# Low-part products last in each half slot, a finer first slot, and turns moved by one product, in a two-layer encoder trunk

## The chip, the core and the metric

The kernel runs on one core of a Trainium2 chip. The metric is the device time of one execution in microseconds (us); the figure for a kernel is the median of its runs. Engines: TensorE (PE; its weight loads are PEld), VectorE (DVE), ScalarE (ACT), GpSimd (POOL), and the DMA queue of SyncE (SP).

## What is computed

An encoder trunk on x of 256 tokens by 2048 features, in float32:

```python
hn = rms_norm(h, mix_norm_g[0]);  h = h + diff_hgrn_mixer(hn, ab_w_in, ab_w_out, ...)   # 8+8 heads
hn = rms_norm(h, mlp_norm_g[0]);  h = h + square(relu(hn @ mlp_w_up[0])) @ mlp_w_down[0]
hn = rms_norm(h, mix_norm_g[1]);  h = h + short_conv_mixer(hn, conv_w_in, conv_w, conv_w_out)
hn = rms_norm(h, mlp_norm_g[1]);  h = h + square(relu(hn @ mlp_w_up[1])) @ mlp_w_down[1]
return rms_norm(h, final_norm_g)
```

The inner width of the MLP is 8192. Nearly all the work is products of 256 tokens with some 420 MB of weights.

## The kernel before, in words

**Split products.** Each operand is split into a high part (rounded to the type fp32r) and a low part (what is left). A product of x and w is the sum of three: high times high, high times low and low times high. ScalarE makes the high part of the weights (`w_hi`, L439 and L563), VectorE the low part (`w_lo`, the subtraction in L450 and L567), TensorE does the three matmuls (L471, L473, L475 in `multiply`, L1137, L1140, L1142 in `product`).

**Slots and half slots.** Weights come in slots of 512 rows by 512 columns (1 MB), 502 in all; a half slot is 256 rows. `w_hi` and `w_lo` are rings of four half slots. The semaphores `hi_ready`, `lo_ready` and `w_used` count half slots: ScalarE's split of one waits until TensorE is through with the one four places before (`w_used`), VectorE's waits for `hi_ready`, and TensorE waits for `lo_ready` before its first matmul of the half slot. `multiply` has 12 matmuls in a half slot (both token tiles), `product` has 6.

**Stages.** First the head projections (a first head written out, then a loop), then the output projection (`OUT_HALVES`, L1667 to L1681 add its result to h), then three stages `stage(st)`: MLP, convolution, MLP. A stage begins with 8 plain slots and goes on in rounds of `ROUND`: P1 D0 P5 D1 P7 D2 P6 D3 P3 D4 P4 D5 P2 D6 D7. P names are the seven products of a Strassen scheme on blocks of the first weight matrix (two slots each, by `product`), D names are slots of the second matrix or of other projections (one slot each, by `multiply`). An MLP stage has seven such rounds (r = 1 to 7), the convolution stage three. For P5, P7, P6 and P4 weight blocks have first to be summed in place (`block_sum`, L1921 on VectorE, the rest as DMAs of POOL's queue), and ScalarE's high part waits for the sum.

**The order** on every engine is written out by hand: the same walk over the names with each engine's tasks put before or after its split of a slot. Around the change these are: `turn` and `conv_turn` (four transposes of a finished block on TensorE, L1195 and L1215), after which ScalarE takes the high part (`hidden_hi`) and VectorE the low part (`hidden_lo`, L1996) or multiplies it into the convolution (`times_b`, L1985); a turn waits until the one before it has been read. `add_block` (L1681) and `add_scaled` (L1667) add a product to h and free its PSUM pair.

**The start.** x comes in four column blocks, each with the DMA of L599, between the weights of slots 0 to 3. TensorE transposes a block (`gain_transpose_pe`, L911), ScalarE and VectorE write its high and low part (`norm_hi_of` L1312, `norm_lo_of` L1650), then slot 0 is multiplied in two halves with the next block's transposes between.

Of the kernel before, what the change touches and what calls it, by code (L numbers as in the profile page):

```python
# [114 lines left out]
COPY_AT = 14  # L115

# [26 lines left out]
def build(nc, x, mix_norm_g, mlp_norm_g, final_norm_g, ab_w_in, ab_w_out, diff_lambda, diff_subln_g,  # L143
          hgrn_lb, hgrn_norm_g, conv_w_in, conv_w, conv_w_out, mlp_w_up, mlp_w_down, out):
    with ExitStack() as ctx:
# [133 lines left out]
        w_used = sem("w_used")  # L279
        x_in = [sem(f"x_in{i}") for i in range(CB)]  # L280
# [119 lines left out]
        def load(sp, base, step, i, src, pieces=1):  # L400
# [8 lines left out]
            for q in range(pieces):  # L409
                sp.dma_start(raw[:, slot, q], src(q)).then_inc(  # L410
                    first_half if isinstance(base, int) and base == 0 and q < 2 else landed[slot], 16)
# [167 lines left out]
        def _(sp):  # L579
# [16 lines left out]
            for p in range(8):  # L596
                if p < CB:
# [298 lines left out]
        def gain_transpose_pe(n, cb):  # L896

            if n == 0:
                nc.tensor.wait_ge(x_in[cb], 16)
# [4 lines left out]
            for b in range(2):  # L904
# [10 lines left out]
        def before_slot(n, j):  # L915

            if n == 0 and j == 0:
                gain_transpose_pe(0, 0)
# [8 lines left out]
        def _(pe):  # L927

            pe.wait_ge(const_pool, 2)
            pe.wait_ge(mix_rows_in, 16)  # L930
# [123 lines left out]
            for c in range(2):  # L1054
                for j in range(4):
                    if c == 0:
# [3 lines left out]
                    if (c, j) == (0, 0):  # L1060
                        head_product(c, j, 0, 0, 0, 0, (0,))
                        gain_transpose_pe(0, 1)
                        head_product(c, j, 0, 0, 0, 0, (1,))
                        continue
# [28 lines left out]
            def stage(st):  # L1093
# [3 lines left out]
                def product(r, name):  # L1097
# [29 lines left out]
                    for k in range(4):  # L1127
# [6 lines left out]
                        pe.wait_ge(lo_ready, 2 * at_slot + k + 1)  # L1134
                        for q in range(2):
# [4 lines left out]
                            nc.tensor.matmul(BANK[name], hi[:, kt], w_lo[:, ring, q],  # L1140
# [1043 lines left out]
```

## Time and profile before

| | |
|---|---|
| median of 3 runs | 2271.85 us (2271.69 to 2272.12) |
| the profiled execution | 2272.94 us |
| its span, first to last instruction | 2271.2 us |
| granted TensorE clock, mean over the span | 0.999 |
| TensorE busy | 2236.9 us, 98% |
| VectorE, ScalarE, POOL busy | 81%, 59%, 13% |
| read from HBM | 422.79 MB, 187 GB/s over the span |

Busy is the time in which an engine works on some instruction; the ends of matmuls are modelled and overlap, so the start-to-start distance of matmuls tells more than their duration. A row of the timeline gives the start, the duration, the instruction and, in brackets, the idle time before it with what released it. Idle time of an engine that nothing waits for costs nothing.

### The profile page before, as it was taken

The numbers are of one execution on the slowest core, as the hardware profiler recorded it, in microseconds if no ns is written. First come the engines' busy times: TensorE is split into PE (matmuls) and PEld (weight loads), VectorE is DVE, ScalarE is ACT, GpSimd is POOL, SyncE is SP. The second block draws the span as 40 slices with busy tenths as digits, with TensorE's granted clock in tenths as the row PEclk, the third lists the DMA queues.
The fourth block names the chain that finished last, engine by engine and source line by source line (L and its number), as shares of the span: only waits on it lengthen the run. The fifth ranks groups of instructions, "written<-read, shape, count | busy, mean of one in ns | idle before, by whom it ended". The sixth has DMA issues, their size and how long they took to land.

```text
span 2271.2 us, 28870 instructions
## 1 busy us (share of the span) xinstructions
PE 2236.9 (98%) x10267; PEld 1833.3 (81%) x10267; DVE 1833.4 (81%) x1952; ACT 1346.2 (59%) x1740; POOL 287.8 (13%) x415
## 2 busy tenths in 40 slices
PE   8999999999999999999999999999999999999998
PEld 6888888878788888888888787788787888888887
DVE  5777788866888888888876988886888888888885
ACT  5555555537666666666556565565665665665664
POOL 4444555520000000000000000000000000000000
PEclk9999999999999999999999999999999999999999
DMA  9555555556778678678656768757687787787755
GB/s 262 168 150 165 148 166 148 148 172 218 209 240 268 198 237 269 198 240 268 199 164 235 239 223 236 230 153 251 187 276 200 228 282 198 226 278 203 224 172 176
DMA packets 326128, 479.89 MB, mean 211 GB/s; under 512 B 13913, under 2 KB 145282, under 8 KB 319362
## 3 DMA queue, kind: packets, MB, share of 16 engines
q1 hardware_dynamic: 318050, 423.88, 57.2%
q0 software_dynamic: 7344, 53.48, 12.7%
q8 instruction: 69, 1.13, 0.2%
q10 hardware_dynamic: 624, 1.07, 0.1%
q14 instruction: 41, 0.34, 0.0%
HBM read 422.79 MB, written 2.10 MB: 187 GB/s over the span
## 4 chain that ended last, share of the span: by engine, by line
PE 82%; DVE 14%; ACT 2%; issue 2%; DMA 0%; POOLq 0%; ACTq 0%; DVEq 0%; POOL 0%
PE pair L471 19%; PE pair L475 18%; PE pair L473 18%; PE m L1137 7%; PE m L1142 7%; PE m L1140 7%; DVE w_lo L567 6%; DVE raw L1921 4%; ACT w_hi L563 2%; DVE h L1667 1%; PE m L979 1%; PE m L1195 1%; PE m L1043 1%; PE m L911 1%; DVE w_lo L450 0%
## 5 line engine op out<-in xcount | busy, mean ns | idle before, releaser
L563 ACT ACTIVATE w_hi<-raw 128x1024 fp32r<-128x1024 f32 x796 | 816.8, 1056 | 625.3 <-DVE raw L1921 292.5
L567 DVE TENSOR_TENSOR w_lo<-raw,w_hi 128x1024 fp32r<-128x1024 f32 x796 | 940.4, 1220 | 244.8 <-ACT w_hi L563 241.3
L471 PE MATMUL pair<-w_hi,yT_hi 128*128 128x512 f32 x1264 | 501.0, 396 | 3.2 <-DVE h L1681 1.0
L475 PE MATMUL pair<-w_hi,yT_lo 128*128 128x512 f32 x1264 | 493.1, 390 | 0.0
L473 PE MATMUL pair<-w_lo,yT_hi 128*128 128x512 f32 x1264 | 492.3, 389 | 0.0
L450 DVE TENSOR_TENSOR w_lo<-raw,w_hi 128x1024 fp32r<-128x1024 f32 x208 | 256.1, 1253 | 136.3 <-ACT w_hi L439 135.0
L439 ACT ACTIVATE w_hi<-raw 128x1024 fp32r<-128x1024 f32 x208 | 217.9, 1059 | 244.2 <-PE pair L475 243.4
L471 PE MATMUL pair<-w_hi,xT_hi 128*128 128x512 f32 x832 | 332.1, 399 | 4.1 <-DVE w_lo L450 3.2
L475 PE MATMUL pair<-w_hi,xT_lo 128*128 128x512 f32 x832 | 325.6, 391 | 0.0
L473 PE MATMUL pair<-w_lo,xT_hi 128*128 128x512 f32 x832 | 325.0, 391 | 0.0
L471 PEld LDWEIGHTS pair<-w_hi,yT_hi 128*128 128x128 f32 x1264 | 237.4, 188 | 56.7 <-issue 7.7
L475 PEld LDWEIGHTS pair<-w_hi,yT_lo 128*128 128x128 f32 x1264 | 237.2, 188 | 50.8
L473 PEld LDWEIGHTS pair<-w_lo,yT_hi 128*128 128x128 f32 x1264 | 237.6, 188 | 46.9
L880 POOL DMA_DIRECT2D raw<-raw x51 | 44.4, 871 | 1328.6 <-DVE raw L1921 885.8
L1137 PE MATMUL m<-w_hi,xT_hi 128*128 128x512 f32 x520 | 202.9, 390 | 0.0
L1142 PE MATMUL m<-w_hi,xT_lo 128*128 128x512 f32 x520 | 202.6, 390 | 0.0
L1140 PE MATMUL m<-w_lo,xT_hi 128*128 128x512 f32 x520 | 202.3, 389 | 0.0
L1921 DVE TENSOR_TENSOR raw<-raw 128x2048 f32<-128x2048 f32 x85 | 192.7, 2284 | 0.0
L471 PEld LDWEIGHTS pair<-w_hi,xT_hi 128*128 128x128 f32 x832 | 156.8, 189 | 38.9 <-issue 5.9
L475 PEld LDWEIGHTS pair<-w_hi,xT_lo 128*128 128x128 f32 x832 | 156.7, 188 | 33.6
L473 PEld LDWEIGHTS pair<-w_lo,xT_hi 128*128 128x128 f32 x832 | 157.0, 189 | 30.5
L1137 PE MATMUL m<-w_hi,tail 128*128 128x512 f32 x408 | 163.6, 401 | 7.4 <-DVE w_lo L567 7.4
(184 smaller groups left out, 2322.5 us busy)
## 6 DMA issues: line engine op xcount, KB each, us to landing
raw<-in_mlp_w_up SPq DMA_DIRECT2D x128, 1024.0 KB, 7.1
raw<-in_mlp_w_down SPq DMA_DIRECT2D x256, 512.0 KB, 6.5
raw<-in_ab_w_in SPq DMA_DIRECT2D x256, 256.0 KB, 4.0
raw<-raw POOLq DMA_DIRECT2D x51, 1024.0 KB, 8.6
raw<-in_conv_w_in SPq DMA_DIRECT2D x32, 1024.0 KB, 6.1
raw<-in_ab_w_out SPq DMA_DIRECT2D x64, 256.0 KB, 4.5
raw<-in_conv_w_in SPq DMA_DIRECT2D x32, 512.0 KB, 4.9
raw<-in_conv_w_out SPq DMA_DIRECT2D x32, 512.0 KB, 5.8
```

The lines of the kernel that those rows point to most:

```text
L439: nc.scalar.activation(w_hi[:, ring], raw[:, raw_slot(base), 2 * k:2 * k + 2], ACT.Copy).then_inc(hi_ready, 1)
L450: nc.vector.tensor_tensor(w_lo[:, ring], raw[:, slot, 2 * k:2 * k + 2], w_hi[:, ring].bitcast(F32), ALU.subtract).then_inc(lo_ready, 1)
L471: nc.tensor.matmul(dst[:, tt], at(hi, kt, tt), w_hi[:, ring, q], start=begin, stop=False)
L473: nc.tensor.matmul(dst[:, tt], at(hi, kt, tt), w_lo[:, ring, q], start=False, stop=False)
L475: mm = nc.tensor.matmul(dst[:, tt], at(lo, kt, tt), w_hi[:, ring, q], start=False, stop=end)
L563: nc.scalar.activation(w_hi[:, entry % HALVES], src, ACT.Copy).then_inc(hi_ready, 1)
L567: nc.vector.tensor_tensor(w_lo[:, entry % HALVES], src, w_hi[:, entry % HALVES].bitcast(F32), ALU.subtract).then_inc(lo_ready, 1)
L880: pool.dma_start(blocks[a][:, 1], blocks[b][:, 1], accum_op=ALU.add).then_inc(added[name], 16)
L1137: nc.tensor.matmul(BANK[name], hi[:, kt], w_hi[:, ring, q], start=kt == 0 and not more, stop=False, skip_group_check=more)
L1140: nc.tensor.matmul(BANK[name], hi[:, kt], w_lo[:, ring, q], start=False, stop=False, skip_group_check=more)
L1142: mm = nc.tensor.matmul(BANK[name], lo[:, kt], w_hi[:, ring, q], start=False, stop=kt == 7, skip_group_check=more)
L1921: nc.vector.tensor_tensor(blocks[a][:, k], blocks[a][:, k], blocks[b][:, k], ALU.add).then_inc(sums.sem, 1)
```

## The change

1. In `multiply` and `product` a half slot's matmuls are put in another order: first all with `w_hi` (8 of 12, or 4 of 6), after a wait for `hi_ready`; then those with `w_lo` (4, or 2), after a wait for `lo_ready`. `w_used` still goes up with the last one. `last_down` stays as it was.
2. The first slot: the first block of x comes in two halves with semaphores of their own, each followed by two quarters of the weights of slot 0. TensorE, ScalarE and VectorE take block and slot in halves. Twelve transposes of the identity into an unused bank come before everything on TensorE, and twelve between the two halves' transposes.
3. Turns: in the MLP stages' first round the turn of C22 comes after D0 (before: after P1), with `hidden_hi` and `hidden_lo` a step later. In the convolution `times_b` of the first tile half comes on VectorE before the second slot's split of P1 (round 2) or P3 (rounds 1 and 3), where it came at D0 or D4. In the output projection VectorE's `add_block` of half 14 comes before its split.

```diff
@@ multiply @@
-                eng.wait_ge(lo_ready, count(2, k + 1, base, step, i))
+                eng.wait_ge(hi_ready, count(2, k + 1, base, step, i))
                 for q in range(2):
                     kt = kt0 + 2 * k + q
                     begin = first and k == ks[0] and q == 0
-                    end = last and k == ks[-1] and q == 1
                     for tt in range(NT):
                         nc.tensor.matmul(dst[:, tt], at(hi, kt, tt), w_hi[:, ring, q],
                                          start=begin, stop=False)
-                        nc.tensor.matmul(dst[:, tt], at(hi, kt, tt), w_lo[:, ring, q],
+                        nc.tensor.matmul(dst[:, tt], at(lo, kt, tt), w_hi[:, ring, q],
                                          start=False, stop=False)
-                        mm = nc.tensor.matmul(dst[:, tt], at(lo, kt, tt), w_hi[:, ring, q],
-                                              start=False, stop=end)
+                eng.wait_ge(lo_ready, count(2, k + 1, base, step, i))
+                for q in range(2):
+                    end = last and k == ks[-1] and q == 1
+                    for tt in range(NT):
+                        mm = nc.tensor.matmul(dst[:, tt], at(hi, kt0 + 2 * k + q, tt),
+                                              w_lo[:, ring, q], start=False, stop=end)
                 mm.then_inc(w_used, 1)
...
@@ SP @@
+                if p == 0:
+                    for k in range(2):
+                        cols = slice(256 * k, 256 * k + 256)
+                        sp.dma_start(h[:, :, cols], x[0].rearrange("(t p) n -> p t n", p=P)[:, :, cols]
+                                     ).then_inc([x_first, x_in[0]][k], 16)
+                        load(sp, 0, 0, 0, head_columns(0, 0, 0), 4, (2 * k, 2 * k + 1))
+                    continue
...
@@ TensorE @@
             pe.wait_ge(const_pool, 2)
+            for _ in range(WARM[0]):
+                nc.tensor.transpose(M[2][:, 0:P], ident[:], ident[:])
...
+                    if (c, j) == (0, 0):
+                        gain_transpose_pe(0, 0, (0,))
+                        for _ in range(WARM[1]):
+                            nc.tensor.transpose(M[2][:, 0:P], ident[:], ident[:])
+                        gain_transpose_pe(0, 0, (1,))
+                        pe.wait_ge(norm_lo[0], 1)
+                        head_product(c, j, 0, 0, 0, 0, (0,))
+                        gain_transpose_pe(0, 1)
+                        pe.wait_ge(norm_lo[0], 2)
+                        head_product(c, j, 0, 0, 0, 0, (1,))
+                        continue
...
-                        if name == "P1":
+                        if name == ("D0" if r == 1 else "P1"):
                             turn(r - 1, "C22" if r == 1 else "C11")
...
@@ ScalarE @@
-            norm_hi_of(0, 0)
-            for n in range(2):
-                split_hi(eng, n, 0, 0)
-                if n == 0:
-                    norm_hi_of(0, 1)
+            for b in range(2):
+                norm_hi_of(0, 0, (b,))
+                split_hi(eng, 0, 0, 0, (b,))
+            norm_hi_of(0, 1)
+            split_hi(eng, 1, 0, 0)
...
-                        if name == "D0":
+                        if name == ("P5" if r == 1 else "D0"):
                             hidden_hi(r - 1, "C22" if r == 1 else "C11")
...
@@ VectorE @@
+                if q == 14:
+                    add_block(cb, OUT_AT + q // 2, 0, 0, q % 2)
                 split_lo(dve, OUT_AT + q // 2 + 2, 0, 0, (q % 2,))
-                if hd == HEADS - 1:
+                if hd == HEADS - 1 and q != 14:
                     add_block(cb, OUT_AT + q // 2, 0, 0, q % 2)
...
-                            if name in (("D0", "P5") if r == 2 else ("D4", "P4")):
-                                times_b(r - 1, int(name[0] == "P"))
+                            if name == ("P5" if r == 2 else "P4"):
+                                times_b(r - 1, 1)
...
+                                if name == ("P1" if r == 2 else "P3"):
+                                    times_b(r - 1, 0)
                                 split(slot + 3)
...
-                        if name == "P1":
+                        if name == ("D0" if r == 1 else "P1"):
                             hidden_lo(r - 1, "C22" if r == 1 else "C11")
```

`product` is changed as `multiply` is, and VectorE's start as ScalarE's.

The order in which TensorE gets its instructions, at a P6 of a later round of the first MLP stage, before (L471 to L475 belong to the slot D2 ahead of it; `tail` holds both parts of P6's left operand):

```order
L471 MATMUL pair<-w_hi,yT_hi 128x512
L473 MATMUL pair<-w_lo,yT_hi 128x512
L475 MATMUL pair<-w_hi,yT_lo 128x512
L1137 MATMUL m<-w_hi,tail 128x512 [waits lo_ready,copied]
L1140 MATMUL m<-w_lo,tail 128x512
L1142 MATMUL m<-w_hi,tail 128x512
L1137 MATMUL m<-w_hi,tail 128x512
L1140 MATMUL m<-w_lo,tail 128x512
L1142 MATMUL m<-w_hi,tail 128x512
L1137 MATMUL m<-w_hi,tail 128x512 [waits lo_ready]
```

and now:

```order
L480 MATMUL pair<-w_lo,yT_hi 128x512 [waits lo_ready]
L480 MATMUL pair<-w_lo,yT_hi 128x512 x3
L1157 MATMUL m<-w_hi,tail 128x512 [waits hi_ready,copied]
L1160 MATMUL m<-w_hi,tail 128x512
L1157 MATMUL m<-w_hi,tail 128x512
L1160 MATMUL m<-w_hi,tail 128x512
L1165 MATMUL m<-w_lo,tail 128x512 [waits lo_ready]
L1165 MATMUL m<-w_lo,tail 128x512
L1157 MATMUL m<-w_hi,tail 128x512 [waits hi_ready]
```

Four of the six matmuls of the half slot now stand ahead of the wait for the low part, and a half slot has two waits.

VectorE in round 2 of the convolution, from the block sums of P5 on (L1985 is `times_b`), before:

```order
L1921 TENSOR_TENSOR raw<-raw 128x2048 [waits lo_ready,landed_b00]
L1921 TENSOR_TENSOR raw<-raw 128x2048 [waits lo_ready,landed_b01]
L567 TENSOR_TENSOR w_lo<-raw,w_hi 128x1024 [waits hi_ready] x2
L1985 TENSOR_TENSOR beside<-m,beside 128x4x128 [waits cv_taps,cv_T]
L567 TENSOR_TENSOR w_lo<-raw,w_hi 128x1024 [waits hi_ready] x2
L1985 TENSOR_TENSOR beside<-m,beside 128x4x128 [waits cv_taps,cv_T]
```

and now (L2010 is `times_b`):

```order
L1946 TENSOR_TENSOR raw<-raw 128x2048 [waits lo_ready,landed_b00]
L1946 TENSOR_TENSOR raw<-raw 128x2048 [waits lo_ready,landed_b01]
L2010 TENSOR_TENSOR beside<-m,beside 128x4x128 [waits cv_taps,cv_T]
L572 TENSOR_TENSOR w_lo<-raw,w_hi 128x1024 [waits hi_ready] x4
L2010 TENSOR_TENSOR beside<-m,beside 128x4x128 [waits cv_taps,cv_T]
```

The first of the two has moved ahead of the two low parts of P5's first slot.

TensorE at the very start, now (before, the transposes of h were one group of eight behind the transpose of `blk`, and no row of identities was there):

```order
L943 MATMUL m<-ident 128x128 [waits const_pool]
L943 MATMUL m<-ident 128x128 x11
L945 MATMUL m<-ident,blk 128x32 [waits mix_rows_in]
L924 MATMUL m<-ident,h 128x128 [waits x_first]
L924 MATMUL m<-ident,h 128x128 x3
L1073 MATMUL m<-ident 128x128 x12
L924 MATMUL m<-ident,h 128x128 [waits x_in0]
L924 MATMUL m<-ident,h 128x128 x3
L471 MATMUL pair<-w_hi,xT_hi 128x512 [waits hi_ready,norm_lo0]
```

Slot 0's first product now needs four transposes of x, not eight, but both groups of twelve and the second four stand ahead of it in the queue.

## Rows read from the trace of the kernel before

**Rows 1.** The page: busy time, share and instructions of each engine.

```profile
PE 2236.9 (98%) x10267; PEld 1833.3 (81%) x10267; DVE 1833.4 (81%) x1952; ACT 1346.2 (59%) x1740; POOL 287.8 (13%) x415
```

**Rows 2.** Windows: stretch, its length, busy us of each engine (x starts), clock, DMA.

```profile
496.00:520.00 24.00, 24.00 (x107) 19.89 (x106) 12.23 (x11) 9.01 (x10) 0.00 (x0) 1.00 0.59 176
```

**Rows 3.** Waits of TensorE: us in total, times, longest us.

```profile
PE m L1137 <- DVE w_lo L567: 7.4, 17, 0.8
PE m L1215 <- DVE beside L1985: 2.8, 3, 1.4
```

**Rows 4.** Timeline of TensorE, one round: start us, us, instruction [idle before].

```profile
764.08 0.39 PE L475 MATMUL pair<-w_hi,yT_lo 128*128 128x512 f32 x1
764.81 0.47 PE L1137 MATMUL m<-w_hi,tail 128*128 128x512 f32 x1 [0.34 <-DVE w_lo L567]
765.12 0.40 PE L1140 MATMUL m<-w_lo,tail 128*128 128x512 f32 x1
...
781.10 0.39 PE L1142 MATMUL m<-w_hi,tail 128*128 128x512 f32 x1
781.61 0.47 PE L471 MATMUL pair<-w_hi,yT_hi 128*128 128x512 f32 x1
...
786.94 0.39 PE L475 MATMUL pair<-w_hi,yT_lo 128*128 128x512 f32 x1
787.30 0.47 PE L1137 MATMUL m<-w_hi,tail 128*128 128x512 f32 x1
787.61 0.39 PE L1140 MATMUL m<-w_lo,tail 128*128 128x512 f32 x1
```

**Rows 5.** Timeline of VectorE in the same round.

```profile
755.45 1.40 DVE L1667 SCALAR_TENSOR_TENSOR h<-pair,rstd,h 128x512 f32<-128x512 f32 x2
...
763.44 2.36 DVE L567 TENSOR_TENSOR w_lo<-raw,w_hi 128x1024 fp32r<-128x1024 f32 x2
...
774.27 4.75 DVE L567 TENSOR_TENSOR w_lo<-raw,w_hi 128x1024 fp32r<-128x1024 f32 x4 [1.13 <-ACT w_hi L563]
...
782.52 2.29 DVE L1921 TENSOR_TENSOR raw<-raw 128x2048 f32<-128x2048 f32 x1
785.93 2.36 DVE L567 TENSOR_TENSOR w_lo<-raw,w_hi 128x1024 fp32r<-128x1024 f32 x2 [1.13 <-ACT w_hi L563]
```

**Rows 6.** Timeline of TensorE: five waits elsewhere.

```profile
489.25 0.50 PE L471 MATMUL pair<-w_hi,yT_hi 128*128 128x512 f32 x1 [0.95 <-DVE h L1681]
...
588.23 0.63 PE L1195 MATMUL m<-ident,blk 128*128 128x128 f32 x4 [0.80 <-DVE yT_lo L1996]
...
1369.91 0.66 PE L1215 MATMUL m<-ident,blk 128*128 128x128 f32 x4 [1.43 <-DVE beside L1985]
...
1398.17 0.50 PE L471 MATMUL pair<-w_hi,yT_hi 128*128 128x512 f32 x1 [0.36 <-DVE w_lo L567]
...
1458.60 0.50 PE L1137 MATMUL m<-w_hi,tail 128*128 128x512 f32 x1 [0.76 <-DVE w_lo L567]
```

**Rows 7.** Timeline of the first slots, all engines.

```profile
5.41 1.97 PE L911 MATMUL m<-ident,h 128*128 128x128 f32 x8 [0.57 <-DMA h<-in_x]
8.14 2.00 ACT L439 ACTIVATE w_hi<-raw 128x1024 fp32r<-128x1024 f32 x2
9.23 2.36 DVE L450 TENSOR_TENSOR w_lo<-raw,w_hi 128x1024 fp32r<-128x1024 f32 x2
10.60 0.76 PE L471 MATMUL pair<-w_hi,xT_hi 128*128 128x512 f32 x1 [3.22 <-DVE w_lo L450]
...
28.18 1.55 ACT L1312 ACTIVATE xT_hi<-m,gains 128x256 fp32r<-128x256 f32 x4
29.64 1.65 DVE L1650 SCALAR_TENSOR_TENSOR xT_lo<-m,gains,xT_hi 128x256 fp32r<-128x256 f32 x4
...
32.94 0.50 PE L471 MATMUL pair<-w_hi,xT_hi 128*128 128x512 f32 x1
```

**Rows 8.** Windows: the first twelve products.

```profile
10.60:15.85 5.25, 5.25 (x12) 3.98 (x13) 0.98 (x1) 0.00 (x0) 0.00 (x0) 1.00 1.16 315
```

More of the change, by code:

```diff
@@ L115 @@
 COPY_AT = 14
+WARM = (12, 12)
 class Steps:
@@ L279, in build @@
         w_used = sem("w_used")
+        x_first = sem("x_first")
         x_in = [sem(f"x_in{i}") for i in range(CB)]
@@ L398, in raw_slot, with load @@
             return raw_at(base) if base < CONV_AT else (0, 1, 6, 7)[raw_at(base)]
-        def load(sp, base, step, i, src, pieces=1):
+        def load(sp, base, step, i, src, pieces=1, of_them=None):
             slot = raw_at(base)
@@ L408, in load @@
                 return
-            for q in range(pieces):
+            for q in of_them or range(pieces):
                 sp.dma_start(raw[:, slot, q], src(q)).then_inc(
@@ L893, in _, with gain_transpose_pe @@
                                         ).then_inc(fin_rstd, 1)
-        def gain_transpose_pe(n, cb):
+        def gain_transpose_pe(n, cb, bs=(0, 1)):
             if n == 0:
-                nc.tensor.wait_ge(x_in[cb], 16)
+                nc.tensor.wait_ge(x_first if bs == (0,) else x_in[cb], 16)
             else:
@@ L903, in gain_transpose_pe @@
                 nc.tensor.wait_ge(pair_read[cb % 2], last - 1 + cb // 2)
-            for b in range(2):
+            for b in bs:
                 if cb:
@@ L915, in before_slot @@
         def before_slot(n, j):
-            if n == 0 and j == 0:
-                gain_transpose_pe(0, 0)
             if j:
@@ L1059, in _ @@
                         transpose_parameters()
[L1060 to L1064, printed above, removed]
                     head_product(c, j, 4 * c + j, 0, 0, 0)
@@ L1133, in product @@
                         ring = (2 * at_slot + k) % HALVES
-                        pe.wait_ge(lo_ready, 2 * at_slot + k + 1)
+                        pe.wait_ge(hi_ready, 2 * at_slot + k + 1)
                         for q in range(2):
@@ L1139, in product @@
                                              skip_group_check=more)
-                            nc.tensor.matmul(BANK[name], hi[:, kt], w_lo[:, ring, q],
+                            nc.tensor.matmul(BANK[name], lo[:, kt], w_hi[:, ring, q],
                                              start=False, stop=False, skip_group_check=more)
-                            mm = nc.tensor.matmul(BANK[name], lo[:, kt], w_hi[:, ring, q],
+                        pe.wait_ge(lo_ready, 2 * at_slot + k + 1)
+                        for q in range(2):
+                            kt = 2 * k + q
+                            mm = nc.tensor.matmul(BANK[name], hi[:, kt], w_lo[:, ring, q],
                                                   start=False, stop=kt == 7,
@@ L1304, in _, with norm_hi_of @@
                           ).then_inc(mix_rows_in, 16)
-            def norm_hi_of(n, cb):
-                for b in range(2):
+            def norm_hi_of(n, cb, bs=(0, 1)):
+                for b in bs:
                     eng.wait_ge(norm_T[n], 2 * cb + b + 1)
@@ L1643, in _, with norm_lo_of @@
         def _(dve):
-            def norm_lo_of(n, cb):
-                for b in range(2):
+            def norm_lo_of(n, cb, bs=(0, 1)):
+                for b in bs:
                     dve.wait_ge(norm_hi[n], 2 * cb + b + 1)
@@ L1856, in parameters_after_exp @@
                 assert step[0] == PAR_LB
-            norm_lo_of(0, 0)
-            for n in range(2):
-                split_lo(dve, n, 0, 0)
-                if n == 0:
-                    norm_lo_of(0, 1)
+            for b in range(2):
+                norm_lo_of(0, 0, (b,))
+                split_lo(dve, 0, 0, 0, (b,))
+            norm_lo_of(0, 1)
+            split_lo(dve, 1, 0, 0)
             for p in range(8):
```

## The prediction

> **What bounds the kernel.** I read the page first: TensorE is busy 2236.9 us of a span of 2271.2 and VectorE, the next, 1833.4 [rows 1]. So only what shortens TensorE's own stream, or its gaps, can count. Then a window without gaps for its pace: 106 weight loads start in 24.00 us, one matmul of 512 columns every 0.226 us [rows 2]. A matmul's recorded 0.39 us overlaps its successor, so a gap costs TensorE about 0.16 us more (0.39 less 0.23) than the idle time in brackets, and I price gaps by start-to-start distances. Rows 2 also tell that a wait that is already met costs nothing: nearly nine half slots lie in that window, each opens with a wait for `lo_ready`, and the pace is that of a stream without waits.
>
> The waits come next. TensorE's gaps are for low parts of weights on VectorE, 7.4 us over 17 (short ones don't show), and for the multiply of the convolution's turns, 2.8 us over three [rows 3]. The timeline shows where. In one round of an MLP stage: before P5 the starts are 764.08 and 764.81, 0.50 over the pace; before D2 781.10 and 781.61, 0.29; before P6 786.94 and 787.30, 0.13 [rows 4]. After each, the second matmul comes 0.31 us after the first instead of 0.23 (764.81 to 765.12), a restart of 0.08. Together 0.50 + 0.29 + 0.13 + 3 x 0.08 = 1.16 us a round, and there are seven such rounds in each of two MLP stages.
>
> Why is the low part late? VectorE's timeline of the same round answers [rows 5]. From 755.45 (the addition to h) it works on without a gap: low parts, two block sums, the low part P5 waits for (first of the pair at 763.44, done at 764.66), and so on to 787.15, when P6's first low part is done (785.93 + 1.22). Its only idle times, 1.13 us each, are for ScalarE's high part, which waits for VectorE's own block sum. So over these 31.7 us VectorE is a chain that doesn't move when TensorE comes earlier; it starts from work that TensorE released well before.
>
> **The change, part by part.**
>
> *Order within a half slot, MLP stages.* Work is only permuted: the same matmuls and loads. The low part is now wanted 4 matmuls (0.91 us) into a half slot of `product`, 8 matmuls (1.81 us) into one of `multiply`. The waits of 0.50 before P5 and 0.29 before D2 are under that and go. Then TensorE comes to P6 at 787.30 - 1.16 + 0.08 = 786.22, does four matmuls, and wants the low part at 787.13. It can't have it before 787.30, as before. So 0.17 us of wait and the restart stay, and what is gained is exactly the four matmuls that now lie ahead of the wait: **0.91 us a round**, not 1.16. The high part that it now waits for is done 1.3 us before the low one, at 785.9, so it doesn't bind. Ring and `w_used` move with TensorE. 14 rounds give 12.7 us. The second wait in 1000 half slots I cost at nothing, by rows 2; bounds below, in the rival.
>
> *Turn of C22 after D0.* The wait there is 0.80 + 0.16 = 0.96 us, once in each MLP stage (at 588.23 [rows 6]). It goes. But the first round's P5 low part, one slot later, hangs on the same unbroken chain of VectorE and takes the gain back. I count 0 beyond the 0.91 of that round (bounds 0 and 1.9). What moves with it: ScalarE's `hidden_hi` now queues ahead of D1's high parts and waits for the turn, VectorE's `hidden_lo` lies ahead of D1's low parts. D1 is two slots of `product` away (24 x 0.226 = 5.4 us) and its place in the ring comes free only a half slot (1.4 us) after the turn, so neither delays anything.
>
> *Convolution.* `times_b` now comes ahead of two low parts (2.36 us for a pair [rows 5]). In round 2 TensorE's turn stood 1.43 + 0.16 us for it (at 1369.91 [rows 6]); the three such waits are 2.8 + 3 x 0.16 = 3.3 us [rows 3]. They go: behind the block sums `times_b` finds its turn long made. The price is that two low parts are 0.68 us later, with 0.9 us of new tolerance. Low parts: the wait at 1398.17 (0.36 + 0.16 + 0.1) is before a D slot and goes, 0.6; round 3 (1458.60 [rows 6]) and round 1 have one chain-bound place each, worth 0.91 by the argument above, 1.8; some 0.2 in small ones. In round 2 TensorE now comes 1.6 us earlier to P7; against the 0.9 of new tolerance I put 0.4 for a wait that arises there, an estimate. Sum 3.3 + 0.6 + 1.8 + 0.2 - 0.4 = 5.5 us (bounds 4 and 8.7, the latter if every wait went).
>
> *Output projection.* The wait at 489.25 is for the addition to h: 0.95 + 0.16, and a restart of 0.1 [rows 6]. The addition no longer stands behind the low part for whose high part VectorE waited. 1.2 us.
>
> *The start.* Slot 0's first product began at 10.60, when VectorE had done the low parts of a whole block of x and the first `w_lo`, though `w_hi` was there at about 9.2 [rows 7]. Now it needs half of x's block and half of the weights: ScalarE can begin its split two activations (0.8 us) earlier, so TensorE starts near 8.0 to 8.5. Then the clock: the first twelve products take 5.25 us, 0.437 each [rows 8], against 0.226; these are TensorE's two levels, 1.2 and 2.4 GHz (the window shows 1.00 granted, but the pace is that of the lower). Before them it had stood idle for 3.22 us. With 24 more transposes before and between it hardly stands, and if that brings it to the upper level another 2.5 us go (12 x 0.21). But the 5 us can't all come through: slot 3 begins at 32.94, and the low part of the fourth block of x that it needs was ready at 31.29, behind ScalarE's unbroken work (28.18, then VectorE at 29.64) [rows 7]. That chain hangs on DMAs that the change doesn't bring earlier (bytes are the same, one DMA more is issued). If it stays, 1.5 us come through; I take it to move up 1.0 and count 2.4 (bounds 1.3 and 5).
>
> One rule speaks against this part. The transposes here ran at the lower level at first: eight took 1.97 us from 5.41 [rows 7], and the level hadn't risen after them. The Trainium skill ("TensorE: Matmul & The Clock Gate", Part 4: PE-mode transpose) says that a transpose doesn't count as activity for the clock in the way a matmul does. By that rule the 24 dummies only take room in the queue and slot 0 runs at 1.2 GHz still; no row here decides it, as no long run of transposes exists.
>
> **Sum.** 12.7 + 5.5 + 1.2 + 2.4 = 21.8 us. Against the profiled execution, 2272.94, that is 2251.1; the median of the runs is 1.1 lower, 2271.85, so I predict **2250.0**.
>
> **The rivals.**
>
> *All waits go.* If VectorE's chain moves up with TensorE, the MLP rounds give their full 14 x 1.16 = 16.2, the turns of C22 1.9, the convolution 8.7, and the start 5: with 1.2 that is 33, or 2239. Against it: rows 5. Chance 0.10.
>
> *The dummies don't warm the array.* Slot 0 then runs at 0.437 a product, and the second twelve dummies, at the lower level 0.2 us each by the eight of rows 7, hold the second transposes up by an estimated 1 us. The start gives 1.3: 2251. Chance 0.30: rows 7 show eight transposes after which the level was still low, but eight are few. It hardly changes the sum, since x's blocks bind behind it.
>
> *The order gives half.* In each MLP round the high part, or a ScalarE copy queued ahead of it, becomes what TensorE waits for; it is ready only 0.3 us before it is now wanted at P6. If it comes 0.75 later, a wait of 0.45 arises and half of the 12.7 goes: 2256. Chance 0.12.
>
> *Slower.* The weight load behind a mid-slot wait can't be fetched ahead while the matmuls in front of it run, and the stream restarts in each of 1000 half slots. A restart costs 0.08 [rows 4]: 80 us, less 22, gives 2330. It decides from 22 ns a half slot. Against it: loads with a wait at the half slot's start lose nothing [rows 2]. Chance 0.03.
>
> **Numbers.** The forecast itself has 0.45; it and the second rival give nearly the same number. 0.2% of this kernel, 4.5 us, is about what a measurement can tell. Only the slower rival and an unseen loss of 18 us or more fall outside "faster": faster 0.95, same 0.02, slower 0.03. The range: from 2250.0 down by 2.6 (start), 2.4 (P6's 0.17 in 14 rounds) and 2 (convolution) to 2243; up by half the MLP part to 2256. It leaves out the first and the last rival.
>
> **What would show it.** In the changed kernel's timeline: matmuls of 512 columns still 0.226 apart; no gap before P5 and D2; in each round one short gap inside P6's first half slot, before its `w_lo` matmuls, ending when VectorE's low part does, with VectorE's unbroken stretch as long as now; no gap at the convolution's turns; slot 0's products beginning near 8 us, 0.226 apart if the dummies work and 0.43 if not; slot 3 near 30.5. A round should take 0.9 us less. A pace over 0.23 in gap-free windows, or gaps before the high-part matmuls, would prove me wrong.

## The result and the profile after

| | before | after |
|---|---|---|
| median | 2272.12 us (6 runs, 2271.69 to 2272.67) | **2250.52 us** (6 runs, 2250.11 to 2250.97) |
| the profiled execution | 2272.94 us, span 2271.2 | 2250.66 us, span 2248.9 |

The ratio is 0.9905, 95% interval 0.9894 to 0.9915. The forecast was 2250.0 in a range of 2243 to 2256. Both profiles have a mean granted clock of 0.999.

Where the time came from is read by comparing the start of the same half slot in the two traces. The differences, by stage:

| stage | gain, us | forecast |
|---|---|---|
| start, up to slot 3 (30.63 for 32.94 [rows 7]) | 2.31 | 2.4 |
| output projection | 1.3 | 1.2 |
| first MLP stage | 6.25 | 6.35 |
| convolution | 6.14 | 5.5 |
| second MLP stage | 6.22 | 6.35 |
| sum | 22.23 | 21.8 |

The sum is from one profiled execution each; the medians are 21.6 apart. Over all matmuls of 512 columns the median distance from start to start is 0.227 us in both traces, so the pace is the same. The page's row of busy engines, for comparison with [rows 1]:

```profile
PE 2232.2 (99%) x10291; PEld 1838.4 (82%) x10291; DVE 1831.8 (81%) x1952; ACT 1338.3 (60%) x1740; POOL 289.5 (13%) x415
```

The work is the same but for 24 transposes. TensorE is busy 4.7 us less although it does the same matmuls: one that is held up, or runs at the lower clock, is recorded longer (0.47 or 0.63 for 0.39 in the rows here). Its waits, against [rows 3]:

```profile
PE m L1165 <- DVE w_lo L572: 2.0, 3, 0.8
PE m L943 <- POOL ident L738: 1.4, 1, 1.4
PE m L924 <- DVE xT_lo L1673: 1.4, 1, 1.4
...
PE m L1157 <- ACT w_hi L568: 0.7, 2, 0.6
```

The 7.4 us over 17 for low parts is 2.0 over 3, and the three waits at turns for `beside` are gone. What is new is small: 0.7 us for high parts. The list leaves short waits out, so the timeline of TensorE has to be read beside it. It is the same round as in [rows 4], now 5.9 us earlier at P5 (L1157 and L1165 are `product`'s high and low parts, L471 and L480 those of `multiply`):

```profile
758.01 1.07 PE L480 MATMUL pair<-w_lo,yT_hi 128*128 128x512 f32 x4
758.91 0.39 PE L1157 MATMUL m<-w_hi,tail 128*128 128x512 f32 x1
759.14 0.39 PE L1160 MATMUL m<-w_hi,tail 128*128 128x512 f32 x1
...
774.78 0.61 PE L1165 MATMUL m<-w_lo,tail 128*128 128x512 f32 x2
775.23 0.39 PE L471 MATMUL pair<-w_hi,yT_hi 128*128 128x512 f32 x1
...
780.67 0.41 PE L1157 MATMUL m<-w_hi,tail 128*128 128x512 f32 x1
...
781.38 0.40 PE L1160 MATMUL m<-w_hi,tail 128*128 128x512 f32 x1
781.78 0.73 PE L1165 MATMUL m<-w_lo,tail 128*128 128x512 f32 x2
782.35 0.40 PE L1157 MATMUL m<-w_hi,tail 128*128 128x512 f32 x1
```

Before P5 (758.91) and D2 (775.23) the pace goes on. At P6 four matmuls now run first, and then the low part is waited for: from 781.38 to 781.78 it is 0.40 us, 0.17 over the pace, and the two low-part matmuls take 0.57 to the next start (782.35), 0.11 over (0.33 or 0.34 between their two starts in each of the 14 rounds). The forecast had 0.17 and 0.08. VectorE in the same round, for [rows 5]:

```profile
750.03 1.40 DVE L1690 SCALAR_TENSOR_TENSOR h<-pair,rstd,h 128x512 f32<-128x512 f32 x2
...
768.85 4.74 DVE L572 TENSOR_TENSOR w_lo<-raw,w_hi 128x1024 fp32r<-128x1024 f32 x4 [1.13 <-ACT w_hi L568]
...
780.50 2.36 DVE L572 TENSOR_TENSOR w_lo<-raw,w_hi 128x1024 fp32r<-128x1024 f32 x2 [1.13 <-ACT w_hi L568]
```

From 750.03 to the end of P6's first low part (780.50 + 1.22) it is 31.69 us, before it was 31.70. The chain has not become shorter, it only begins earlier with everything else; TensorE's wait sits at its end as it did.

The start, for [rows 7, 8], as all engines show it:

```profile
7.86 0.48 PE L471 MATMUL pair<-w_hi,xT_hi 128*128 128x512 f32 x1
8.18 0.39 PE L473 MATMUL pair<-w_hi,xT_lo 128*128 128x512 f32 x1
8.41 0.39 PE L471 MATMUL pair<-w_hi,xT_hi 128*128 128x512 f32 x1
...
18.87 2.01 ACT L441 ACTIVATE w_hi<-raw 128x1024 fp32r<-128x1024 f32 x2 [2.99 <-DMA raw<-in_ab_w_in]
20.79 1.55 ACT L1335 ACTIVATE xT_hi<-m,gains 128x256 fp32r<-128x256 f32 x4
...
25.12 1.99 ACT L441 ACTIVATE w_hi<-raw 128x1024 fp32r<-128x1024 f32 x2
27.02 1.55 ACT L1335 ACTIVATE xT_hi<-m,gains 128x256 fp32r<-128x256 f32 x4
28.48 1.65 DVE L1673 SCALAR_TENSOR_TENSOR xT_lo<-m,gains,xT_hi 128x256 fp32r<-128x256 f32 x4
...
30.18 0.14 PEld L953 LDWEIGHTS m<-ident,blk 121*128 121x128 f32 x1 [0.53 <-DVE xT_lo L1673]
...
30.63 0.50 PE L471 MATMUL pair<-w_hi,xT_hi 128*128 128x512 f32 x1
```

The first products come 0.23 us apart, the upper level, and the first half slot is 5.3 us earlier than it was (11.50 for 16.84 at the second). But at slot 3 only 2.31 are left: ScalarE waits until 18.87 for slot 2's weights to land, and from there it works without a gap until the fourth block of x is scaled; TensorE waits for that block's low part (30.18).

### The profile page after: what moved, and what is told of

It reads as the page before. It is cut to its first block, busy times and chain, and to the rows that moved or that the text cites. A ratio compares the mean times of both kernels' runs of the same rounds, so it can differ in the third digit from the quotient of the medians.

```text
span 2248.9 us, 28920 instructions
## 1 busy us (share of the span) xinstructions
PE 2232.2 (99%) x10291; PEld 1838.4 (82%) x10291; DVE 1831.8 (81%) x1952; ACT 1338.3 (60%) x1740; POOL 289.5 (13%) x415
## 4 chain that ended last, share of the span: by engine, by line
PE 92%; DVE 5%; ACT 1%; issue 1%; SPq 0%; DMA 0%; POOLq 0%; POOL 0%; ACTq 0%; DVEq 0%
PE pair L471 20%; PE pair L473 20%; PE pair L480 20%; PE m L1165 9%; PE m L1157 9%; PE m L1160 9%; DVE w_lo L572 2%; DVE raw L1946 1%; PE m L1218 1%; PE m L993 1%; PE m L1057 1%; ACT w_hi L568 0%; DVE w_lo L452 0%; PE m L924 0%; PE m L1007 0%
## 5 line engine op out<-in xcount | busy, mean ns | idle before, releaser
L471 PE MATMUL pair<-w_hi,yT_hi 128*128 128x512 f32 x1264 | 499.6, 395 | 0.0
L480 PE MATMUL pair<-w_lo,yT_hi 128*128 128x512 f32 x1264 | 338.2, 389 | 0.0
L471 PE MATMUL pair<-w_hi,xT_hi 128*128 128x512 f32 x832 | 331.1, 398 | 0.0
L480 PEld LDWEIGHTS pair<-w_lo,yT_hi 128*128 128x128 f32 x1264 | 237.3, 188 | 50.0
L471 PEld LDWEIGHTS pair<-w_hi,yT_hi 128*128 128x128 f32 x1264 | 237.5, 188 | 48.3 <-DVE yT_lo L1840 0.5
L480 PE MATMUL pair<-w_lo,xT_hi 128*128 128x512 f32 x832 | 222.9, 390 | 0.0
L1157 PE MATMUL m<-w_hi,xT_hi 128*128 128x512 f32 x520 | 202.8, 390 | 0.0
L471 PEld LDWEIGHTS pair<-w_hi,xT_hi 128*128 128x128 f32 x832 | 156.4, 188 | 34.0 <-issue 2.3
L480 PEld LDWEIGHTS pair<-w_lo,xT_hi 128*128 128x128 f32 x832 | 156.1, 188 | 33.3 <-DVE w_lo L572 0.3
L1157 PE MATMUL m<-w_hi,tail 128*128 128x512 f32 x408 | 160.1, 392 | 0.9 <-ACT w_hi L568 0.7
L1165 PE MATMUL m<-w_lo,xT_hi 128*128 128x512 f32 x520 | 160.3, 389 | 0.0
```

Source lines behind the costliest of these rows:

```text
L480: mm = nc.tensor.matmul(dst[:, tt], at(hi, kt0 + 2 * k + q, tt), w_lo[:, ring, q], start=False, stop=end)
L1157: nc.tensor.matmul(BANK[name], hi[:, kt], w_hi[:, ring, q], start=kt == 0 and not more, stop=False, skip_group_check=more)
L1165: mm = nc.tensor.matmul(BANK[name], hi[:, kt], w_lo[:, ring, q], start=False, stop=kt == 7, skip_group_check=more)
```

## Experiments

Each kernel's median is of 4 to 11 executions, taken beside the kernel before (whose medians are 2272.29 to 2272.50 in the four groups). In brackets stand the ratio to that kernel and its 95% interval; the intervals of neighbouring kernels overlap, but the executions of each kernel in the table lie within 1.3 us of each other. Differences under 1 us between medians are not read as effects. The gains by stage, from the traces, in the same way as above:

| kernel | median, us | start | output | MLP 1 | conv. | MLP 2 |
|---|---|---|---|---|---|---|
| after | 2250.52 | 2.31 | 1.31 | 6.25 | 6.14 | 6.22 |
| order alone | 2255.59 | 2.28 | 0.05 | 6.32 | 2.67 | 6.33 |
| all but the order | 2266.90 | 2.19 | 1.32 | 0.12 | 2.55 | 0.09 |
| wait at the head | 2267.45 | 1.92 | 1.29 | -0.39 | 2.38 | -0.47 |
| two matmuls ahead | 2258.06 | 2.28 | 1.30 | 3.33 | 4.87 | 3.05 |
| eight ahead | 2247.65 | 2.29 | 1.31 | 8.00 | 5.96 | 7.79 |
| longer chain | 2258.56 | 2.43 | 1.32 | 2.29 | 6.13 | 2.21 |
| `times_b` back | 2253.82 | 2.31 | 1.32 | 6.42 | 2.68 | 6.45 |
| C22 back | 2250.32 | 2.00 | 1.31 | 6.50 | 6.21 | 6.16 |
| no dummies | 2250.61 | 2.18 | 1.29 | 6.49 | 6.15 | 6.17 |
| new start | 2248.14 | 4.41 | 1.33 | 6.39 | 6.14 | 6.36 |
| new start, no dummies | 2249.73 | 2.88 | 1.30 | 6.34 | 6.14 | 6.19 |
| new start, eight ahead | **2245.58** | 3.97 | 1.33 | 8.02 | 5.98 | 7.91 |

Outside the start the same edits give the same stage gain within 0.3 us in all of them, so differences of 0.5 and more can be read there. With the same edits the start varies by 0.5 (1.92 to 2.43), with the landings: ScalarE's split of slot 2 begins at 18.87 in the changed kernel and at 19.27 in the one with 1.92.

### The change in two halves

The kernel before with the new order and its waits alone:

> The kernel before with nothing of the change but the new order of the matmuls inside a half slot and its second wait. Theory (the order saves four matmuls, 0.91 us, at the one place of a round where TensorE waits for a split, because VectorE's chain up to that split is of fixed length): 14 MLP rounds x 0.89 = 12.5, the low parts of the convolution 2.6 to 2.8, so 2272.1 - 15.2 = 2257, with the three turns' waits in the convolution (2.8 us in all) still there. Rival (the moved turns and adds of the other parts carry the gain, the order only a share): above 2263.

And the changed kernel without them:

> The changed kernel with the matmuls of a half slot in their old order and its one wait: only the start, the turns, the products with b and the output's addition are left of the change. Theory: start 2.3, addition 1.3, turns of the convolution 3.3 to 3.5, the turn of C22 in the MLPs nothing, so 2272.1 - 7.0 = 2265. Rival (C22's turn gives 0.95 in each MLP, as its wait in the trace of the kernel before suggests): 2263. Together with the run of the order alone it shows whether the parts add up: the two gains should sum to 21.6 within 1 us.

Measured: 2255.59 (ratio 0.9926, 0.9912 to 0.9939) and 2266.90 (0.9975, 0.9966 to 0.9985). The MLP stages are all order: 6.3 each with it, 0.1 without. The gains of the two halves add to 22.2 by the medians, near the whole's 21.6, but the table shows that this is partly luck (by the traces it is 23.9 for 22.2). The start is counted twice: either half gives all of it (2.28, 2.19). And the convolution gives less in the halves (2.67 + 2.55) than in the whole (6.14). Without the order the turns gain 0.94, 1.47 and 0.94, and in round 2 a new wait for low parts takes 0.7 back within the next 16 half slots; with the order the second turn gives 1.67 and nothing is taken back. So the wait that the prediction put at 0.4 exists, but the new order covers it. Both forecasts of this section missed by more than 1 us, 2257 mainly because it left the start's 2.28 out, and 2265 in part because it counted the convolution's turns at 3.3 to 3.5.

Without the order, C22's turn gains 1.22 us by the start of D0 and P5's low part takes 1.21 back in the very next slot. Part of both is the turn's own four transposes, which now come behind D0 and not ahead of it.

### Is it the order of the matmuls, or where the wait stands?

```diff
                 eng.wait_ge(hi_ready, count(2, k + 1, base, step, i))
+                eng.wait_ge(lo_ready, count(2, k + 1, base, step, i))
```

(and the same in `product`.)

> The changed kernel, with the matmuls in the new order, but with a wait for w_lo also ahead of the first high-part matmul, so that a half slot again begins only when both parts are there. Theory: neither the permutation nor a wait that is met costs or gives anything, so this is the kernel without the order's gain, 2265 as in the run of everything but the order, within 0.7 us of it. Rival (an executed wait costs TensorE its start, about 1000 of them more here): at 10 ns each 2275. Rival (the permutation itself, three matmuls on one weight tile's neighbours, changes the pace): the mean spacing of 512-column matmuls leaves 226 ns.

The median is 2267.45 (0.9978, 0.9969 to 0.9987), 0.55 above the kernel without the order. With both waits at the head the whole gain is gone, so the permutation is worth nothing by itself and what counts is that the wait stands later. This kernel has two waits more in a half slot than the one without the order, the high part's and the second one for the low part, some 2000 in all. They and the permutation together cost 0.55 by the medians, with overlapping runs, and 1.4 by the two profiled spans; the traces don't show it spread over the half slots: between the waiting places the gain stays constant, and 0.07 a round is lost at P6. What these 0.07 are stayed open.

### How much is a matmul ahead of the wait worth?

Two ahead, in `product`:

```diff
-                        pe.wait_ge(lo_ready, 2 * at_slot + k + 1)
-                        for q in range(2):
-                            kt = 2 * k + q
+                            if q == 0:
+                                pe.wait_ge(lo_ready, 2 * at_slot + k + 1)
                             mm = nc.tensor.matmul(BANK[name], hi[:, kt], w_lo[:, ring, q],
```

> The changed kernel, but in the activation products of the MLPs and the convolution the wait for w_lo stands after two matmuls of a half slot and not after four (each weight tile's three matmuls then follow each other). The multiply of the down projections stays as changed. Theory (P6 gains exactly the matmuls that lie ahead of its wait, since the chain behind it doesn't move): 2 x 0.226 = 0.45 us a round are given back, 14 x 0.45 = 6.3 us, and 1 to 2 of the convolution, so 2258. Rival (the wait only has to be later than some point, and the number of matmuls doesn't matter): 2250.5. Together with none ahead (2267.45), four (2250.5) and eight (2247.65) it gives the gain as a function of the matmuls ahead: the first two should be worth about as much as the next two, the last four less, since the wait has run out.

Eight ahead, with two half slots taken together in `product`:

```diff
-                    for k in range(4):
+                    for kk in range(2):
...
+                        for k in (2 * kk, 2 * kk + 1):
...
+                            pe.wait_ge(hi_ready, 2 * at_slot + k + 1)
...
+                        for k in (2 * kk, 2 * kk + 1):
...
+                            pe.wait_ge(lo_ready, 2 * at_slot + k + 1)
```

> The changed kernel, with the same idea taken one step further in the activation products of the MLPs and the convolution: the high-part matmuls of two half slots (eight), then the low-part ones of both (four), so that the low part of the first half slot is wanted eight matmuls after the start of the pair and not four. Theory (what is left in P6 is a wait of 0.25 us and 0.08 of restart, in each of 14 rounds, for a chain of fixed length): all of it goes, 14 x 0.33 = 4.6 us, so 2246. Rival 1 (the chain's next wait, the second half slot's high part or the next slot, takes it back): no change, 2250.5. Rival 2 (the first half slot's weight buffer is given back later, by four matmuls or 0.9 us, so ScalarE's and VectorE's splits three slots ahead start later): slower, 2253 or more, with gaps ahead of high-part matmuls.

Measured 2258.06 (0.9938, 0.9924 to 0.9952) and 2247.65 (0.9891, 0.9876 to 0.9906). With two ahead the list of waits has this:

```profile
PE m L1164 <- DVE w_lo L572: 7.8, 19, 1.0
```

and the timeline of TensorE, at P6 of the round shown above, this:

```profile
781.99 0.39 PE L1160 MATMUL m<-w_hi,tail 128*128 128x512 f32 x1
782.66 0.50 PE L1164 MATMUL m<-w_lo,tail 128*128 128x512 f32 x1 [0.28 <-DVE w_lo L572]
783.00 0.40 PE L1157 MATMUL m<-w_hi,tail 128*128 128x512 f32 x1
```

782.66 - 781.99 is 0.45 over the pace, where four ahead have 0.17. Another 0.15 of the loss stands in P5, in two short delays that four ahead don't have. The same place with eight ahead:

```profile
781.80 0.39 PE L1161 MATMUL m<-w_hi,tail 128*128 128x512 f32 x1
782.03 1.14 PE L1168 MATMUL m<-w_lo,tail 128*128 128x512 f32 x4
783.01 0.39 PE L1158 MATMUL m<-w_hi,tail 128*128 128x512 f32 x1
```

The low parts follow at the pace (782.03 - 781.80 = 0.23). By the MLP columns of the table, over 14 rounds, the first two matmuls are worth (6.38 - 0.21) / 14 = 0.44 us a round, the next two (12.47 - 6.38) / 14 = 0.43, and the last four together 0.24. The 0.21 is that of the kernel without the order, so the first step also holds the new order of `multiply`, which all three have; counted from the wait at the head it is 0.52. The first two pairs pay about their own length, 0.45, and then the wait has run out. That is the signature of a chain of fixed length. The forecast of 0.33 for the last step was high, since 0.07 and 0.11 of small delays stay behind in the low-part groups of P6. The buffers that are given back later cost 0.2 us in the convolution and nothing in the MLPs.

### Is VectorE's chain really what binds?

One operation more on VectorE in each MLP round, which nothing waits for:

```diff
+                        if name == "D1":
+                            nc.vector.tensor_reduce(spare[:, ...],
+                                ident[:].unsqueeze(1).broadcast_to([P, 4, P]), AX_X, ALU.add)
```

> The changed kernel with one operation more on VectorE in each of the 14 MLP rounds, between D1 and the splits for P6, a sum over 512 elements per partition that nobody waits for (some 0.6 us by the neighbouring operations of that size; its duration is to be read from the trace). Theory (VectorE's chain up to P6's low part is unbroken and sets P6's start in every round): the time rises by its whole duration in each round, 14 x 0.6 = 8 us, so 2259. Rival (VectorE has slack somewhere in the chain, since it is busy for 81% of the span only, and the gain came from a shorter or earlier chain): less than 2 us, below 2252.5.

The median is 2258.56 (0.9939, 0.9926 to 0.9953). The timeline of the same round, first VectorE, then ScalarE and TensorE at P6:

```profile
774.50 0.68 DVE L2147 TENSOR_REDUCE spare<-ident 128x4 f32<-128x512 f32 x1
775.10 1.40 DVE L1692 SCALAR_TENSOR_TENSOR h<-pair,rstd,h 128x512 f32<-128x512 f32 x2
...
781.00 5.80 ACT L570 ACTIVATE w_hi<-raw 128x1024 fp32r<-128x1024 f32 x6 [5.96 <-DVE raw L1948]
...
782.20 0.47 PE L1159 MATMUL m<-w_hi,tail 128*128 128x512 f32 x1 [0.37 <-ACT w_hi L570]
```

and the list of TensorE's waits:

```profile
PE m L1159 <- ACT w_hi L570: 6.2, 15, 0.6
```

The operation moves its successor by 0.60 us (775.10 - 774.50), 8.4 in 14 rounds; the time rose by 8.04. An engine that is busy for 81% of the span hands on 96% of what is added to it here. The lesson for reading is in the releaser: TensorE now waits for ScalarE's `w_hi`, and ScalarE was idle for 5.96 us before it, until VectorE's block sum. The wait list names the last link, not the one that is late.

### The turns

Undone one at a time:

```diff
-                            if name == ("P5" if r == 2 else "P4"):
-                                times_b(r - 1, 1)
+                            if name in (("D0", "P5") if r == 2 else ("D4", "P4")):
+                                times_b(r - 1, int(name[0] == "P"))
...
-                                if name == ("P1" if r == 2 else "P3"):
-                                    times_b(r - 1, 0)
```

> The changed kernel with one part undone: VectorE's products with b in the convolution stand at their old places again, ahead of the splits of D0 and D4. Theory (VectorE's place in its queue made TensorE wait at the three turns of the convolution, 0.94, 1.67 and 0.93 gained there): 2250.5 + 3.5 = 2254, with those three gaps back. Rival (the new order of the matmuls alone would have covered them): 2250.5 to 2251.

```diff
-                        if name == ("D0" if r == 1 else "P1"):
+                        if name == "P1":
                             turn(r - 1, "C22" if r == 1 else "C11")
```

(and `hidden_hi` and `hidden_lo` moved back in the same way.)

> The changed kernel with one part undone: the turn of C22 and the hidden values made of it stand at their old places in the first round of each MLP. Theory (TensorE's wait at that turn is absorbed, since P5's low part is bound by VectorE's chain in any case and takes it back within the same round): 2250.5, within 0.3. Rival (the wait of 0.95 before the turn counts in each MLP): 2252.4.

`times_b` back: 2253.82 (0.9919, 0.9905 to 0.9932), 3.3 us back, and the convolution's gain falls from 6.14 to 2.68, by 3.46. The three waits are in the list again:

```profile
PE m L1238 <- DVE beside L2010: 2.9, 3, 1.4
```

C22 back: 2250.32 (0.9902, 0.9887 to 0.9918), the same as the changed kernel, in a trace in which the wait of [rows 6] is back (timeline of TensorE):

```profile
584.93 0.63 PE L1218 MATMUL m<-ident,blk 128*128 128x128 f32 x4 [0.80 <-DVE yT_lo L2021]
...
591.54 0.39 PE L1160 MATMUL m<-w_hi,tail 128*128 128x512 f32 x1
591.77 0.62 PE L1165 MATMUL m<-w_lo,tail 128*128 128x512 f32 x2
```

In the changed kernel's timeline the turn has no wait and P5's low part has one:

```profile
590.24 0.40 PE L1160 MATMUL m<-w_hi,tail 128*128 128x512 f32 x1
591.19 0.73 PE L1165 MATMUL m<-w_lo,tail 128*128 128x512 f32 x2 [0.56 <-DVE w_lo L572]
```

It is one wait or the other, 0.80 at the turn or 0.56 at P5's low part: this part of the change moves a wait and removes none.

### The start

```diff
-WARM = (12, 12)
+WARM = (0, 0)
```

> The changed kernel without the 24 transposes of the identity on TensorE at its start. Theory (they raise the granted clock before the first product, but from the second slot on the start is bound by landings and by ScalarE's and VectorE's chain): TensorE stays at its lower level through the first slot, its matmuls 0.43 us apart and not 0.23, a loss of up to 2.4 us there of which slots 1 to 3 take back more than half, so 2250.5 + 0.2 to 1.1 = 2251. Rival (the loss stays): 2253. Rival (the transposes do nothing for the clock): 2250.5 and the same pace in the first slot as with them.

The median is 2250.61 (0.9904, 0.9889 to 0.9919), no loss, although the timeline of TensorE shows a slower first slot:

```profile
8.28 0.78 PE L471 MATMUL pair<-w_hi,xT_hi 128*128 128x512 f32 x1
8.86 0.63 PE L473 MATMUL pair<-w_hi,xT_lo 128*128 128x512 f32 x1
9.28 0.63 PE L471 MATMUL pair<-w_hi,xT_hi 128*128 128x512 f32 x1
...
14.28 0.47 PE L471 MATMUL pair<-w_hi,xT_hi 128*128 128x512 f32 x1
```

The first products are 0.43 us from start to start, the lower level, and the second half slot begins 2.8 us later than with the dummies. In the changed kernel the transposes alone come before the first product:

```profile
1.43 2.82 PE L943 MATMUL m<-ident 128*128 128x128 f32 x12 [1.43 <-POOL ident L738]
...
5.33 2.30 PE L1073 MATMUL m<-ident 128*128 128x128 f32 x12
7.47 0.63 PE L924 MATMUL m<-ident,h 128*128 128x128 f32 x4
```

The transposes' starts are 0.21 us apart up to 7.03, in the middle of the second twelve, and 0.11 from there on. The loss of the kernel without them doesn't last: slot 2 begins at 24.52 for 24.36, slot 3 at 30.78 for 30.63. The order alone, with the old start, comes to slot 3 at 30.68, in this timeline of ScalarE:

```profile
14.61 1.57 ACT L1318 ACTIVATE xT_hi<-m,gains 128x256 fp32r<-128x256 f32 x4 [4.56 <-PE m L914]
...
18.70 2.01 ACT L439 ACTIVATE w_hi<-raw 128x1024 fp32r<-128x1024 f32 x2 [0.62 <-DMA raw<-in_ab_w_in]
```

So neither the finer first slot nor the clock set the start's gain; ScalarE's work behind the landing at 18.87 does. If that is so, another order of this work must give what the change couldn't:

```diff
-                if p in (1, 2):
-                    norm_hi_of(0, p + 1)
-                    squares(0, (2 * p - 2, 2 * p - 1))
+                if p < 2:
+                    norm_hi_of(0, p + 2)
...
                 split_hi(eng, p + 2, 0, 0)
+                if p in (1, 2):
+                    squares(0, (2 * p - 2, 2 * p - 1))
```

(and `norm_lo_of` moved in the same way on VectorE.)

> The changed kernel with a new order in its start on ScalarE and VectorE: the third and fourth block of x are scaled (hi and lo) ahead of the weights' splits of slots 2 and 3, and ScalarE's squares of the blocks come after those splits. Theory (with or without the change's edits slot 2 begins at 24.4 and slot 3 at 30.6, because ScalarE's work behind the landing of slot 2's weights at 18.9 is in the wrong order, not because of TensorE or its clock): slot 2 begins right behind slot 1 and its transposes, at 23.0, slot 3 at 28.9, 1.7 us earlier, and it stays: 2248.8. Rival (DMA landings bind slots 2 and 3): slot 3 stays at 30.6 or moves by less than 0.5, 2250.3. Rival (VectorE's sum of the squares, now waiting longer, delays a split behind it): a gap of its own at slot 4 or 5, 2250 or more.

The median is 2248.14 (0.9895, 0.9880 to 0.9910), 2.4 us below the changed kernel, where 1.7 was expected. The timeline of ScalarE and TensorE:

```profile
16.11 1.57 ACT L1335 ACTIVATE xT_hi<-m,gains 128x256 fp32r<-128x256 f32 x4
18.98 2.01 ACT L441 ACTIVATE w_hi<-raw 128x1024 fp32r<-128x1024 f32 x2 [1.30 <-DMA raw<-in_ab_w_in]
22.48 1.57 ACT L1335 ACTIVATE xT_hi<-m,gains 128x256 fp32r<-128x256 f32 x4 [1.49 <-PE m L924]
...
22.64 0.48 PE L471 MATMUL pair<-w_hi,xT_hi 128*128 128x512 f32 x1
...
28.56 0.50 PE L471 MATMUL pair<-w_hi,xT_hi 128*128 128x512 f32 x1
```

The weights land at the same time (18.98), but the third block of x is scaled by then, and ScalarE has slack. Slot 2 begins at 22.64 and slot 3 at 28.56, each 0.3 to 0.4 earlier than expected. Now the dummies' cover is gone, so they should count:

> The kernel with the new order of the start, without the 24 transposes of the identity on TensorE. Without them the changed kernel lost nothing (2250.61 against 2250.52), because ScalarE's chain held slot 2 at 24.4 in any case. Theory (that chain was the cover, and here it is gone): slot 0 at the lower clock ends later, slot 1 begins at 17.9 instead of 16.3, and slot 2 right behind it at 24.3 instead of 22.6, a loss of 1.65 us that stays, so 2248.14 + 1.65 = 2249.8. Rival (slot 2 is bound by another chain still): 2248.1 to 2248.5.

The median is 2249.73 (0.9900, 0.9883 to 0.9917), so 1.6 us are lost where the changed kernel lost none. In the trace slot 2 begins at 24.19 for 22.64. With four executions each (2249.04 to 2250.25, and 2248.01 to 2248.76 with the dummies) the sign is clear and the size rough, since the second half of x's first block also landed some 0.8 us later in this trace.

### Both further steps

> Both further steps together: the high-part matmuls of two half slots ahead of their low-part ones, and the new order of ScalarE and VectorE in the start. Theory (they act at different places and add up): 2250.5 - 2.9 - 1.7 = 2246. Rival (one of the two gains is noise or is absorbed): 2247.6 or more.

The median is 2245.58 (0.9883, 0.9868 to 0.9898), 4.9 us below the changed kernel and 26.7 below the one before. The steps gave 2.9 and 2.4 alone, 5.3 if they added up. The stages agree with the single runs but for the start (3.97 for 4.41), where x lands later: the transposes of its third block begin at 15.89, for 15.42 with the new start alone, both behind a wait for the DMA.

## Why the prediction was right

- **What bounds the kernel** held. The pace stayed (0.227 before and after), gaps ended where VectorE's chain did, and the longer chain shows its length to be what counts.
- **Order, MLP stages**: 12.47 for 12.7. The working (the matmuls ahead of the wait, not the sum of the waits) is what two, four and eight ahead confirm. That the number is so near is partly luck. In the round of [rows 4] the delays before are 1.32 and not 1.16, since later restarts of 0.07 in P5 (at 767.9) and 0.09 in P6 (at 790.4) weren't counted, and 0.42 and not 0.25 stay: the wait of 0.17, a restart of 0.11 and not 0.08, 0.11 at the next low-part group and 0.03 at P6's head. The difference is 0.90 a round, for 0.91.
- **C22 at nothing** held: C22 back is no slower.
- **Convolution**: 6.14 for 5.5, the one term off by more than a tenth. The step that failed is the 0.4 for a wait that arises in round 2, an estimate: it arises only without the new order (0.7 there). The turns gave 0.94 + 1.67 + 0.93 = 3.5 for 3.3; the rest is as worked out, 0.90 and 0.97 at the two chain-bound places for 0.91 each, 0.53 for 0.6.
- **Output projection**: 1.3 for 1.2.
- **The start**: 2.31 for 2.4, the right size from a partly wrong share. The 1.0 by which the chain was "taken to move up" was a guess, and 1.5 + 1.0 is 2.5, not 2.4. Measured, the fourth block's low part begins 1.16 earlier (28.48 for 29.64) and the time from there to slot 3 is 1.15 shorter. The order alone gives the whole 2.28: TensorE's earlier end of slot 0 lets ScalarE scale the second block at 14.6 and not 16.7, and from then on ScalarE stands at the landing near 18.7.
- **The rival on the dummies** fell, with its rule. The changed kernel's first products are 0.23 us apart and those without dummies 0.43, with nothing else changed, and the step from 0.21 to 0.11 between transposes comes before any product, so these transposes do raise TensorE to its upper level. The Trainium skill ("TensorE: Matmul & The Clock Gate", Part 4: PE-mode transpose) says of transpose mode that it doesn't count as PE-busy in the same way. This case's trace doesn't agree, as far as these float32 transposes, recorded as MATMUL, run in that mode, which no trace here shows. The measurement decides. That it hardly changes the sum held: 0.1 us.
- **All waits go** fell at four matmuls ahead, but with eight ahead the MLP stages give 15.8 of the 16.2 that this rival had.
- **Half, slower**: both fell. High parts made TensorE wait 0.7 us in all, and the pace of 0.227 shows no loss at mid-slot waits that are met.

## What to carry to other kernels

Where a consumer waits for the later of two inputs, put all work that needs only the earlier one first. Over a stretch in which the producer's chain doesn't move, the gain is the smaller of two things: all the waits in it together, with their restarts (1.16 us a round by the prediction's count), and the work that now lies ahead of the last of them (0.91). So price the work ahead, not only the waits listed, and ask what the next wait on that chain takes back. A cost that is hidden is worth removing only together with its cover: the dummies were worth nothing until ScalarE's work was put in order, and 1.6 us then.

## What was not expected of the hardware

- Transposes of 128 columns alone bring TensorE to its upper level before the first product. The windows print a granted clock of 1.00 at the lower level too ([rows 8] is such a window), but that is no reading: the trace's record of the clock begins only at 7.02 us in the changed kernel, at 13.39 without the dummies and at 16.26 in the kernel before, and just there the starts draw together (transposes from 0.21 to 0.11 apart). Before that point only the distance of the starts tells the level.
- After a wait in the middle of a half slot the next start comes 0.11 over the pace, at the head of a half slot 0.08.
